# Loading half of the value pages of a paged attention cache from a second engine's queue

## What is computed

```
k_past = cache_k[l, page_table].reshape(dec_b, past, N_ATT_HEADS, ATT_V_DIM)
v_past = cache_v[l, page_table].reshape(dec_b, past, N_ATT_HEADS, ATT_V_DIM)
...
w = diff_weights(s, rel_bias(q_pos, k_pos, table), lam)
return (jnp.einsum('bhqk,bkhe->bqhe', w[..., :P], v_past)
        + jnp.einsum('bhqk,bkhe->bqhe', w[..., P:], v_new))
```

## Time and profile before

| | us |
|---|---|
| median of 3 runs (2135.77 to 2137.03) | 2136.57 |
| profiled execution, its own time | 2137.1 |
| its span, first to last instruction | 2135.4 |

### The profile page before, as it was taken

The page is one execution under the profiler, slowest core; times in us unless marked ns, Lnnn a source line. Parts: engine busy times, 40 slices in busy tenths (PEclk is TensorE's granted clock), DMA queues, the critical chain, the costliest instruction groups (busy, mean ns, idle before and its releaser), DMA issues.

```text
span 2135.4 us, 32009 instructions
## 1 busy us (share of the span) xinstructions
PE 1901.5 (89%) x12993; PEld 1685.9 (79%) x12993; DVE 973.0 (46%) x1126; ACT 500.5 (23%) x761; POOL 68.2 (3%) x77
## 2 busy tenths in 40 slices
PE   6699997998787797899897896999999999999994
PEld 5699894665444597779773794999999999999992
DVE  2625787884543625742320328434323333224445
ACT  3321104665322412130332214111000000001122
POOL 0000001000000000100101002000000000000001
PEclk7899998999888898999999898999999999999995
DMA  5312116665477121411115112111112111111004
GB/s 158 122 40 66 52 59 187 198 184 159 144 229 221 61 80 56 141 57 42 59 40 194 63 40 101 40 39 59 40 39 59 39 39 60 39 40 54 29 15 162
DMA packets 141092, 187.17 MB, mean 88 GB/s; under 512 B 7752, under 2 KB 99082, under 8 KB 140486
## 3 DMA queue, kind: packets, MB, share of 16 engines
q1 hardware_dynamic: 131248, 137.52, 21.6%
q0 software_dynamic: 9072, 47.75, 6.2%
q10 hardware_dynamic: 686, 0.73, 0.1%
HBM read 165.65 MB, written 20.74 MB: 87 GB/s over the span
## 4 chain that ended last, share of the span: by engine, by line
PE 80%; DVE 7%; ACT 4%; DMA 4%; issue 2%; SPq 1%; POOL 0%; DVEq 0%; POOLq 0%; ACTq 0%
PE PS L1462 19%; PE PS L1463 19%; PE PS L1464 19%; PE PS L1452 7%; PE PS L1539 2%; PE PS L1600 2%; PE PS L1646 2%; PE PS L1620 2%; DMA bias_rows<-BVEC 2%; PE PS L1857 1%; PE PS L1833 1%; PE PS L1477 1%; PE PS L1817 1%; PE PS L1478 1%; PE PS L1479 1%
## 5 line engine op out<-in xcount | busy, mean ns | idle before, releaser
L1462 PE MATMUL PS<-XH,WH 128*128 128x352 f32 x1992 | 643.1, 323 | 0.0
L1463 PE MATMUL PS<-XL,WH 128*128 128x352 f32 x1992 | 638.4, 321 | 0.0
L1464 PE MATMUL PS<-XH,WL 128*128 128x352 f32 x1992 | 637.9, 320 | 0.0
L995 DVE CAST WH<-RAW 128x1024 fp32r<-128x1024 f32 x128 | 96.9, 757 | 720.4 <-PE PS L1464 694.5
L1463 PEld LDWEIGHTS PS<-XL,WH 128*128 128x128 f32 x1992 | 374.2, 188 | 0.0
L1462 PEld LDWEIGHTS PS<-XH,WH 128*128 128x128 f32 x1992 | 373.7, 188 | 0.0
L1464 PEld LDWEIGHTS PS<-XH,WL 128*128 128x128 f32 x1992 | 373.3, 187 | 0.0
L997 DVE TENSOR_TENSOR WL<-RAW,WH 128x1024 fp32r<-128x1024 f32 x128 | 158.9, 1242 | 4.4
L1110 DVE SCALAR_TENSOR_TENSOR CY<-GP,DW,CY 128x1024 f32<-128x1024 f32 x124 | 158.7, 1280 | 1.0 <-DVE CY L1113 1.0
L1462 PE MATMUL PS<-HH,WH 128*128 128x352 f32 x462 | 149.0, 323 | 0.0
L1463 PE MATMUL PS<-HL,WH 128*128 128x352 f32 x462 | 148.1, 321 | 0.0
(11 more groups left out here) (299 smaller groups left out, 2334.2 us busy)
## 6 DMA issues: line engine op xcount, KB each, us to landing
PG<-in_cache_k SPq DMA_DIRECT2D x128, 256.0 KB, 3.0
PG<-in_cache_v SPq DMA_DIRECT2D x128, 256.0 KB, 3.0
RAW<-in_w_gate SPq DMA_DIRECT2D x22, 512.0 KB, 4.0
RAW<-in_w_up SPq DMA_DIRECT2D x22, 512.0 KB, 5.2
RAW<-in_w_in SPq DMA_DIRECT2D x20, 512.0 KB, 4.7
h_spill<-H POOLq DMA_DIRECT2D x2, 4224.0 KB, 13.9
H<-h_spill POOLq DMA_DIRECT2D x2, 4224.0 KB, 13.4
CKV<-in_cache_mem_k POOLq DMA_DIRECT2D x8, 1024.0 KB, 5.4
```

Source lines behind the costliest of these rows:

```text
L995: dve.tensor_copy(WH[v % 2][:, :, :], raw).then_inc(hi_done, 1)
L1462: pe.matmul(out, WH[u][:, k, :], xh[:, k, cols], start=(k == 0), stop=False)
L1463: pe.matmul(out, WH[u][:, k, :], xl[:, k, cols], start=False, stop=False)
L1464: mm = pe.matmul(out, WL[u][:, k, :], xh[:, k, cols], start=False, stop=(k == kt - 1))
```

## The change

SP loads all 16 pages of sequence 0 as before, and from sequence 1 on only the even ones. ACT loads the odd pages of sequences 1 to 7, four at the end of each of the slots 1 to 14, behind the exponential of map 1: slot s loads pages 1, 3, 5 and 7 of slot s + 1. Each load waits for v_used as on SP. ACT also waits once, before its slots, for the page table.

```diff
@@ -486,7 +486,7 @@
             for b in range(DB):
-                for r in range(PAGES):
+                for r in range(0, PAGES, 2 if b else 1):
                     if b:
                         sp.wait_ge(v_used, PAGES * (b - 1) + r + 1)
@@ -831,6 +831,8 @@
+            n_pages = io["cache_v"].shape[1]
+            act.wait_ge(pt_in, 16)
             for s, (h, qb) in enumerate(order):
@@ -842,6 +844,15 @@
                 att_exp(h, qb, 1)
+                first = 8 * (s - 2 * QT) + 8
+                for n in range(first + 1, first + 8, 2):
+                    if first < 16 or n >= DB * PAGES:
+                        continue
+                    b, r = n // PAGES, n % PAGES
+                    act.wait_ge(v_used, PAGES * (b - 1) + r + 1)
+                    page = act.value_load(PT[:, PAGES * b + r:PAGES * b + r + 1], min_val=0, max_val=n_pages - 1)
+                    src = io["cache_v"][0].rearrange("n s h d -> n s (h d)")[ds(page, 1), :, :]
+                    act.dma_start(PG[:, r, :], src.rearrange("n s d -> (n s) d")).then_inc(pg_in[r], 16)
```

## The result

The changed kernel takes 2142.07 us, the median of 20 runs (2134.61 to 2148.5), against 2134.84 us for the kernel before (20 runs on the same chips). The ratio is 1.0034, with an interval of 1.0025 to 1.0044. That is +7.2 us, where +5.7 was forecast.

What follows compares the result with a forecast made beforehand. Value-page loads (15.0% of the stretch's chain) and SP's issue lines (11.7%), one page per 1.12 us, were taken as the bound. Slots -1.0, clock +4, transfers +1, w_out +1.7 gave +5.7 on 2137.1, median 2142 us; range 2129 to 2157.

Steps and rivals of the forecast that it cites:

- SP leaves the chain: Value stage: with 56 of 112 issues gone, SP needs 4.5 us a slot, less than any slot lasts; gain in short slots.
- ACT issues late, not behind the exponential, and it does not run ahead: End of each slot: ACT's first register load comes 0.03 us after the OSB copy starts, its DMA issue 0.72 us later.
- The third case: Rival: ACT's issues start only when the exponential has finished, adding 12 us over 12 slots, giving 2154 us; chance 0.12.
- Page 1 sets the gap at 5.25 us in the long slots: From OSB to WT: page 1 starts 4.35 us after OSB, WT 0.90 later; +6.35 in slots 2 to 5, +4.26 in 10 to 12.
- the landing of 3.6 us: Page 1 on ACT's queue: time from DMA issue to landing, median 3.0 before, lengthened by SP's even page sent beside it.
- the hold of ACT's queue: Behind OSB: four issues occupy ACT's queue until 4.5 us, hidden since WT comes at 5.25; no cost of its own.
- Pages 3, 5 and 7 don't bind, and the short slots gain 11.6 us: Short slots and last pages: only page 1 is late; -2.25 in slots 6 and 7, -6.99 in 13 to 15.
- The terms for what is left out: Additions to the slot sum of -1.0 us: clock +4, transfers +1, w_out loaded beside odd pages of slots 14 and 15 +1.7.
- The clock's +4: Slots 7, 13 and 15: values run at half clock after waits for pages, +4 us, bounds 0 and 8.
- the transfers' +1: Four short slots: eight pages ask 6.9 us of engine time where slots should last 6.6 to 6.8; +1 us, bounds 0 and 2.
- The price of 6.9 us for the transfers of a slot: Short slots: eight pages at 0.86 us of engine time each; transfers alone would hold a slot at 6.9 us.
- the last rival: ACT's queue runs ahead and issues odd pages early; only transfers hold short slots, 11 us gained, 2125 us; chance 0.05.

## Why the prediction held, and where it did not

The forecast was 2142 us, the measurement 2142.07. That they meet to 0.1 us is luck: the forecast started from three runs whose median lay 1.7 us above that of all 20, and its change was 1.5 us too small. Inside the change, too, part is the right mechanism and part is errors that met. Per group of slots, from the profiled executions (the forecast without the terms for clock, transfers and w_out, which it did not assign to single groups but for w_out):

| us | before | after | change | forecast |
|---|---|---|---|---|
| slots 2 to 5 | 26.26 | 33.65 | +7.4 | +6.35 |
| slots 6 and 7 | 15.65 | 17.24 | +1.6 | -2.25 |
| slots 8 and 9 | 24.10 | 22.76 | -1.3 | -0.8 |
| slots 10 to 12 | 21.24 | 23.84 | +2.6 | +4.26 |
| slots 13 to 15 | 27.50 | 27.41 | -0.1 | -6.99 |
| last page | 2.73 | 1.27 | -1.5 | -1.58 |

**SP leaves the chain.** Right: its lines are gone from the chain's shares. But the gain that hung on this in the short slots did not come, as told below.

**ACT issues late, not behind the exponential, and it does not run ahead.** Right: the first DMA leaves 0.67 to 0.70 us behind OSB (forecast 0.75), except in slot 2 (0.92) and in the first slot of head 3, where it is 0.26 us ahead of it. The third case (2 us behind) and the last (ahead of OSB) fell with that. The step from issue to issue is 1.06 us.

**Page 1 sets the gap at 5.25 us in the long slots.** Right as a mechanism in five of the seven long slots, mis-sized in the landing. The gaps were 4.94, 5.35, 4.45 and 4.67 us in slots 2 to 5 and 4.61, 4.44 and 4.47 in slots 10 to 12, 4.70 in the mean. The term that was too long is the landing of 3.6 us: page 1, the first on its queue, lands in a median of 2.9. (A landing of 3.0 beside two queues was one of the signs of being wrong. The first of four showed it, the other three did not.) The term behind it was too short: from landing to WT it is 1.07 us and not 0.90, since page 1 alone took 0.41 us behind a wait (573.26) and not half of the 0.55 of a pair. So 0.69 + 2.9 + 1.07 is 4.7. The prediction had called the hold of ACT's queue hidden even under a landing of 2.6 us, though by its own figures (WT at 4.25, the queue held to 4.5) the queue then comes last. That happened in slots 2 and 10, where page 1 landed in 2.66 and 2.74 us and WT stood behind the fourth issue. From WT to OSB slots 2 to 4 kept 3.64, 3.21 and 2.99 us (3.65, 3.22, 2.88 before), as the prediction had it. In slot 5 it took 4.40 us instead of 1.86, by page 3 and the clock, and in slots 11 and 12 page 3 added another 0.6 together. So the gaps were 3.8 us shorter than forecast, the rest 3.2 us longer, and the long slots lost 7.4 + 2.6 = 10.0 us where 10.6 were forecast.

**Pages 3, 5 and 7 don't bind, and the short slots gain 11.6 us.** This step failed. Page 3 binds in the short slots: it lands in 4.1 us in the median, more than the 3.6 of the formula, and in 4.20 and 4.42 us in slots 5 and 7. There the values end when page 3 has come, not when WT has. The short slots 6, 7 and 13 to 15 together became 1.5 us longer, where -9.2 us were forecast, and slot 5, which I had counted among the long ones, took 9.07 us where 7.11 were expected. Slots 13 to 15 took 27.4 us, outside the 20 to 25 that I had named as a sign of being right. The run without even pages shows where it comes from: without them beside the odd ones the kernel is 13 us faster, most of it in short slots. So the late odd pages did not outweigh a gain in the short slots, as the forecast had it; there was no gain to outweigh.

**The terms for what is left out.** They had to make up 1.5 + 9.2 = 10.7 us in the short slots and had 6.7. The clock's +4 and the transfers' +1 stood in the right place (I charged half clock to three slots and 0.25 us of transfer to four), but how the 10.7 divide among page 3, the clock and w_out no run shows; the run in which w_out waits is too coarse to tell a term of 1.7 from nothing. The forecast survived because 4.0 us too little in the short slots met 0.6 too much in the long ones, 0.5 too much in slots 8 and 9, and 1.2 us less in slots 0 and 1 (16.07 us, before 17.22), which the change doesn't reach and which I don't explain: 5.7 + 4.0 - 0.6 - 0.5 - 1.2 = 7.4, the stage's +7.5.

**The price of 6.9 us for the transfers of a slot**, on which the last rival's 2125 us rested, was no floor for a slot. The price of a page was about right: with the engines 0.95 busy, 315 and 334 GB/s are 0.83 and 0.78 us for 256 KB, near the 0.86 of the earlier trace rows, and 6.7 and 6.3 us for eight pages. What failed is the step from there to the length of a slot: with sixteen pages of lead slots of 8 pages took 4.4 to 6.5 us, as part of their pages had come during longer slots. That rival's mechanism, pages far enough ahead, is what the two kernels with sixteen pages of lead have, and they reached 2119.66 and 2106.34 us.

**A rule of the Trainium skill** ("DMA: Bandwidth & Descriptors", section "Issuing engines are not separate DMA queues") has a second issuing engine save only the time to start the DMAs, usually small beside the DMA itself. For this kernel the runs disagree with "usually small": with the lead kept, moving a quarter of the issues to another queue saved 1.3%. Each page cost SP 1.12 us of register load and issue, more than its transfer took at the rate reached later (256 KB at 315 GB/s, 0.83 us).

**What stays open.** How much of the short slots' loss is the clock and how much the wait itself: in the two runs with sixteen pages of lead the granted clock of the first head's short slots was 1.00 with hardly a wait for a page, against 0.74 with them in the changed kernel, but no run held the one and moved the other. How much of the long slots' loss is the hold and how much the lateness is not measured apart either, beyond which of the two came last in each slot. Nor is it shown why one kernel's slots 8 and 9 are shorter than another's.

## What to carry to other kernels

Moving part of a stream of loads to a second queue does help where the first queue's issue is the pace, but a load belongs on the queue whose instruction list reaches it early: ask of each issue what lead it has in microseconds in the shortest stage, not in buffers. Give the busy engine few issues, of the data that is wanted last, and as far ahead as the buffers allow: here two a slot, two slots ahead, gave 0.987, where four a slot, one slot ahead, gave 1.0034. And an issue on a computing engine is not free even where it never waits: each held ACT's queue for 1.06 us, and what stood behind the fourth was on the chain wherever the pages came in time.

## What was unexpected of the hardware

The landing of a page went with how many pages were under way, more than with how many queues sent them, and by an amount that decided the short slots: 3.0 us from one queue with two others under way, 2.9 for the first and 4.0 to 4.4 for the later of four when SP's queue sends too, 3.9 to 4.8 with both queues far ahead, and 3.0 again without the even pages. In the run with GpSimd behind OSB two queues sent as well, and SP's pages still landed in 3.0. A GpSimd issue of the same page took 0.54 us on the engine (ACT 0.35) with 1.15 to 1.24 us from issue to issue, and landed a little later than SP's beside it (medians of 4.4 and 4.2 us with eight pages of lead, 3.6 and 3.0 behind OSB). Behind a semaphore of ACT its first DMA came 1.57 us after the start of that ACT instruction in most slots; ACT's own, standing in its list behind the same copy, 0.69.
